# A hybrid decoder layer: the final norm of the prompt rows is moved ahead of the last two expert blocks, and the rows of those two blocks are gathered, normed and stored once more

## The reference

```python
h = x + (gc * conv_out + gg * gla_out) @ w_out
h = h + hier_moe(rms_norm(h, norm_ffn), ...)      # each row goes to TOP_K = 2 of 32 experts
# hier_moe: y = segment_sum(yb * row_wt[:, None], row_tok), expert(x) = (silu(x @ w_g) * (x @ w_u)) @ w_d
y_prompt = rms_norm(hp, norm_final)               # (1, 1024, 1024)
y_sample = rms_norm(hs, norm_final)               # (8, 4, 1024)
# rms_norm(x, g) = x * rsqrt(mean(x * x) + EPS) * g, per row
```

## Time and profile before

| what | value |
|---|---|
| median of 3 runs | 1723.63 us (1722.59 to 1725.98) |
| the profiled execution | 1724.93 us |
| its span | 1723.3 us |
| TensorE busy | 1660.8 us, 96% of the span |
| VectorE (DVE), ScalarE (ACT) busy | 1256.2 us (73%), 922.2 us (54%) |
| GpSimd (POOL) busy | 243.3 us (14%) |
| HBM read, written | 325.19 MB, 61.22 MB |

### The profile page before, as it was taken

One profiled execution on the slowest core, in us unless ns is written; L12 is line 12 of the kernel. 1 busy time (PEld: TensorE's weight loads), 2 busy tenths in 40 slices (PEclk: granted clock), 3 DMA queues, 4 the chain that ended last, 5 costly groups with the idle time before them and its releaser, 6 DMA issues.

```text
span 1723.3 us, 24970 instructions
## 1 busy us (share of the span) xinstructions
PE 1660.8 (96%) x8996; PEld 1461.6 (85%) x8996; DVE 1256.2 (73%) x2086; ACT 922.2 (54%) x1177; POOL 243.3 (14%) x266
## 2 busy tenths in 40 slices
PE   8999999999999999999999989999999999999992
PEld 7999987777999999879988878888888888878881
DVE  5234899986766577645554559998989888888893
ACT  6263122217333344336343347878888887787883
POOL 4100111110000000011001223411111111121210
PEclk9999999999999999999999999999999999999996
DMA  5402223241342333356443339999999999999975
GB/s 202 144 26 75 75 99 109 93 117 54 112 125 92 92 92 116 118 170 202 150 160 111 102 153 368 362 374 368 369 392 384 386 382 395 373 370 378 364 262 208
DMA packets 104033, 367.08 MB, mean 213 GB/s; under 512 B 14509, under 2 KB 58753, under 8 KB 90128
## 3 DMA queue, kind: packets, MB, share of 16 engines
q1 hardware_dynamic: 80976, 308.76, 48.2%
q0 software_dynamic: 22768, 57.19, 10.2%
q10 hardware_dynamic: 208, 0.08, 0.0%
HBM read 325.19 MB, written 61.22 MB: 224 GB/s over the span
## 4 chain that ended last, share of the span: by engine, by line
PE 88%; DMA 5%; DVE 3%; ACT 2%; issue 1%; DVEq 0%; SPq 0%; ACTq 0%; POOLq 0%
PE bank L1023 84%; DMA wraw_down<-in_w_expert_down 3%; PE bank L1478 2%; PE bank L1502 1%; DMA uo<-in_x_prompt 1%; DVE gwork L2030 1%; DMA fbuf<-h_scr 1%; PE bank L1395 0%; PE bank L1242 0%; DMA h_scr<-ybuf,kdT 0%; ACT L1582 0%; DVE wL_down L2030 0%; ACT ybuf L1582 0%; ACTq L1599 0%; DVE fbuf L2673 0%
## 5 line engine op out<-in xcount | busy, mean ns | idle before, releaser
L2030 DVE TENSOR_TENSOR wL_down<-wraw_down,wH_down 128x1024 fp32r<-128x1024 f32 x140 | 162.0, 1218 | 29.7 <-ACT wH_down L1582 29.5
L2030 DVE TENSOR_TENSOR wL_up<-wraw_up,wH_up 128x2048 fp32r<-128x2048 f32 x72 | 161.5, 2284 | 23.9 <-ACT wH_up L1582 23.9
L1582 ACT ACTIVATE wH_up<-wraw_up 128x2048 fp32r<-128x2048 f32 x72 | 134.0, 1909 | 68.3 <-DMA wraw_up<-in_w_expert_up 46.8
L2030 DVE TENSOR_TENSOR wL_gate<-wraw_gate,wH_gate 128x2048 fp32r<-128x2048 f32 x72 | 161.7, 2287 | 11.0 <-ACT wH_gate L1582 10.8
L2155 DVE SCALAR_TENSOR_TENSOR ybuf<-uo,gwork,ybuf 128x1024 f32<-128x1024 f32 x120 | 153.6, 1280 | 6.1 <-issue 6.1
L1582 ACT ACTIVATE wH_down<-wraw_down 128x1024 fp32r<-128x1024 f32 x140 | 136.5, 1052 | 14.1 <-DMA wraw_down<-in_w_expert_down 13.9
L967 POOL DMA_INDIRECT h_scr<-ybuf,kdT x36 | 77.0, 2139 | 436.2 <-ACT ybuf L1582 417.5
L1582 ACT ACTIVATE stage<-bank 128x512 f32<-128x512 f32 (+3 forms) x65 | 34.5, 547 | 189.9 <-PE bank L1023 180.3
L1582 ACT ACTIVATE wH_gate<-wraw_gate 128x2048 fp32r<-128x2048 f32 x72 | 134.5, 1933 | 1.2 <-DMA wraw_gate<-in_w_expert_gate 1.2
L1023 PE MATMUL bank<-nTH,gateH 128*128 128x352 f32 x384 | 129.5, 337 | 0.6 <-issue 0.6
L1023 PE MATMUL bank<-nTH,slabH 128*128 128x352 f32 x384 | 124.9, 325 | 1.2 <-ACT uo L1582 0.7
(11 more groups left out here) (334 smaller groups left out, 4251.6 us busy)
## 6 DMA issues: line engine op xcount, KB each, us to landing
wraw_gate<-in_w_expert_gate SPq DMA_DIRECT2D x36, 2048.0 KB
wraw_up<-in_w_expert_up SPq DMA_DIRECT2D x36, 2048.0 KB, 16.3
wraw_down<-in_w_expert_down SPq DMA_DIRECT2D x36, 2048.0 KB
slab_raw<-in_w_in SPq DMA_DIRECT2D x7, 2048.0 KB, 9.3
gate_scr<-stage POOLq DMA_DIRECT2D x16, 528.0 KB, 3.5
vr_scr<-stage POOLq DMA_DIRECT2D x32, 256.0 KB, 2.3
gate_raw<-in_w_in SPq DMA_DIRECT2D x16, 512.0 KB, 8.7
vrbuf<-vr_scr SPq DMA_DIRECT2D x16, 512.0 KB, 6.9
```

Of the source, the lines that this page charges most:

```text
L1582: return act.activation(out, in_, func, **kw)
L2030: return dve.tensor_tensor(out, x, y, op)
```

## The change

The eight prompt tiles are no longer loaded after everything has been scattered, but as soon as `scatter(n-2)` has landed, n being the last block. At that point the rows lack only what blocks n-1 and n add. They go into the raw gate and up buffers of block n-1, which are spent once its up product is done, are normed there, in `flush`, and are stored from there. The scatters of blocks n-1 and n wait until the eight loads have landed. After both scatters POOL gathers the rows of the last two lists from `h_scr` anew, ACT and DVE norm them, and POOL stores them by list over what was stored before, after the eight stores have landed. The sample rows are loaded, normed and stored once, after `moe_done`. The buffer `fbuf` is gone, and so is the one ACT instruction ahead of the tail that brought in the root's table. The diff, cut to its core:

```diff
+        def prompt_tiles(b):
+            return [wraw[1 - b][k][:, D * q:D * (q + 1)] for k in range(2) for q in range(4)]
+        late_rows = [flat(ybuf)[:, D * k:D * (k + 1)] for k in range(2)]
+        sample_rows = xg[0]
 # SP
             def load_last_down(n, j):
                 sp.wait_ge(ed_done, n - 1)
                 load_w(sp, W_DOWN, expert_of(j), n % 2)
+                tiles = prompt_tiles(n % 2)
+                sp.wait_ge(eu_done, n)
+                sp.wait_ge(y_scattered[n % 2], 16 * (n // 2))
+                for t in range(NCH):
+                    sp.dma_start(tiles[t], h_scr[t * P:(t + 1) * P, :]).then_inc(tile_loaded[t], 16)
+                for t in range(NCH):
+                    sp.wait_ge(f_made, t + 1)
+                    sp.dma_start(o["y_prompt"][0, t * P:(t + 1) * P, :], tiles[t]).then_inc(f_out, 16)
...
             sp.wait_ge(moe_done, 1)
-            for t in range(NT):
-                sp.dma_start(fh[t][0:rows(t), :], h_scr[t * P:t * P + rows(t), :]).then_inc(tile_loaded[t], 16)
-            for t in range(NT):
-                sp.wait_ge(f_made, t + 1)
-                dst = ...
-                sp.dma_start(dst, fo[t][0:rows(t), :]).then_inc(f_out, 16)
+            sp.dma_start(sample_rows[0:S_T, :], h_scr[SEQ:T, :]).then_inc(tile_loaded[NCH], 16)
+            sp.wait_ge(f_out, 16 * NCH)
+            sp.wait_ge(f_made, NT)
+            sp.dma_start(o["y_sample"].rearrange("b s d -> (b s) d"), sample_rows[0:S_T, :]).then_inc(f_out, 16)
             sp.wait_ge(f_out, 16 * NT)
+            sp.wait_ge(listed_rows, 16 * 5)
 # POOL
             def all_scattered(n):
+                for t in range(NCH):
+                    pool.wait_ge(tile_loaded[t], 48)
+                scatter(n - 1)
                 scatter(n)
                 pool.wait_ge(y_scattered[n % 2], 16 * (n // 2 + 1))
                 pool.sem_inc(moe_done, 1)
+                for k in range(2):
+                    pool.indirect_dma_start(out=late_rows[k], in_=h_scr, in_offset=<lst_tok[:, n - 1 + k]>,
+                                            bounds_check=T - 1).then_inc(listed_rows, 16)
+                pool.wait_ge(f_out, 16 * NCH)
+                for k in range(2):
+                    pool.wait_ge(f_made, NT + k + 1)
+                    pool.wait_ge(listed_rows, 16 * (3 + k))
+                    pool.indirect_dma_start(out=o["y_prompt"][0], in_=late_rows[k], out_offset=<the same list>,
+                                            bounds_check=SEQ - 1).then_inc(listed_rows, 16)
             def pool_block(n):
-                scatter(n - 1)
                 if n + 1 < NE:
-                    return
-                if n + 1 < NBLK:
-                    maybe(pool, n_more > n + 1 - NE, pool.nop, lambda: all_scattered(n))
+                    scatter(n - 1)
+                elif n + 1 < NBLK:
+                    maybe(pool, n_more > n + 1 - NE, lambda: scatter(n - 1), lambda: all_scattered(n))
 # ACT
+            def row_roots(x, unread, total, root):
+                r = x.shape[0]
+                f(unread[0:r, :], x, ACT.Square, accum_out=total[0:r, :])
+                act.drain()
+                f(root[0:r, :], total[0:r, :], ACT.Sqrt, scale=1.0 / D, bias=eps_t[0:r, :]).then_inc(rms_made, 1)
                 def flush():
                     weight_high(W_DOWN, b, i * 16 + 16, wH[W_GATE])
                     hidden_high(n, last_hidden(1 - b)[0])
+                    squares(0, 2)
                     last_y()
+                    squares(2, 4)
                     take_y(n, b, i * 16, bank=2)
+                    squares(4, NCH)      # squares: wait for tile_loaded[t], row_roots(prompt_tiles(b)[t], ...)
...
-            f(rstd9[0], eps_t, ACT.Sqrt)
-            for t in range(NT):          # the same three instructions, on fh[t]
+            act.wait_ge(tile_loaded[NCH], 48)
+            row_roots(sample_rows[0:S_T, :], xjunk, ss9[NCH], rstd9[NCH])
+            act.wait_ge(listed_rows, 16 * 3)
+            for k in range(2):
+                row_roots(late_rows[k], xjunk, ss[k], rstd[k])
 # DVE
                 def flush():
...
                     hidden_low(n, last_hidden(1 - b))
+                    dve.wait_ge(norm_row_loaded, 32)
+                    for t in range(NCH):
+                        final_norm(t, prompt_tiles(b)[t], rstd9[t])   # reciprocal, then the product, in place
...
-            for t in range(NT):          # reciprocal and product, fh[t] to fo[t]
+            final_norm(NCH, sample_rows[0:S_T, :], rstd9[NCH])
+            for k in range(2):
+                final_norm(NT + k, late_rows[k], rstd[k])
```

More of the change, by code:

```diff
@@ L201, in hybrid_layer @@
         hidTL = at("hidTL", O_Y + R16 // 2 + KB2, [P, FC, P], FR)
-        fbuf = at("fbuf", O_A, [P, 2, NT, D])
         def flat(t):
@@ L370, in hybrid_layer @@
         ey_taken = sem("ey_taken")
-        more_rows = sem("more_rows")
+        listed_rows = sem("listed_rows")
         y_scattered = [sem(f"y_scattered{b}") for b in range(2)]
@@ L444, in hybrid_layer @@
         cnt = small[:, 32:32 + NE]
-        fh = [fbuf[:, 0, t, :] for t in range(NT)]
-        fo = [fbuf[:, 1, t, :] for t in range(NT)]
+        def prompt_tiles(b):
+            return [wraw[1 - b][k][:, D * q:D * (q + 1)] for k in range(2) for q in range(4)]
+        late_rows = [flat(ybuf)[:, D * k:D * (k + 1)] for k in range(2)]
+        sample_rows = xg[0]
         nfin = mtab[:, :]
@@ L777, in _ @@
             sp.wait_ge(moe_done, 1)
-            for t in range(NT):
-                sp.dma_start(fh[t][0:rows(t), :], h_scr[t * P:t * P + rows(t), :]).then_inc(tile_loaded[t], 16)
-            for t in range(NT):
-                sp.wait_ge(f_made, t + 1)
-                dst = o["y_prompt"][0, t * P:t * P + P, :] if t < NCH else o["y_sample"].rearrange("b s d -> (b s) d")
-                sp.dma_start(dst, fo[t][0:rows(t), :]).then_inc(f_out, 16)
+            sp.dma_start(sample_rows[0:S_T, :], h_scr[SEQ:T, :]).then_inc(tile_loaded[NCH], 16)
+            sp.wait_ge(f_out, 16 * NCH)
+            sp.wait_ge(f_made, NT)
+            sp.dma_start(o["y_sample"].rearrange("b s d -> (b s) d"), sample_rows[0:S_T, :]).then_inc(f_out, 16)
             sp.wait_ge(f_out, 16 * NT)
+            sp.wait_ge(listed_rows, 16 * 5)
             sp.wait_ge(state_out, 4 * 16)
@@ L975, in all_scattered @@
                 pool.sem_inc(moe_done, 1)
+                for k in range(2):
+                    pool.indirect_dma_start(out=late_rows[k], out_offset=None, in_=h_scr,
+                                            in_offset=bass.IndirectOffsetOnAxis(
+                                                ap=lst_tok[:, n - 1 + k:n + k], axis=0),
+                                            bounds_check=T - 1, oob_is_err=False).then_inc(listed_rows, 16)
+                pool.wait_ge(f_out, 16 * NCH)
+                for k in range(2):
+                    pool.wait_ge(f_made, NT + k + 1)
+                    pool.wait_ge(listed_rows, 16 * (3 + k))
+                    pool.indirect_dma_start(out=o["y_prompt"][0], in_=late_rows[k], in_offset=None,
+                                            out_offset=bass.IndirectOffsetOnAxis(
+                                                ap=lst_tok[:, n - 1 + k:n + k], axis=0),
+                                            bounds_check=SEQ - 1, oob_is_err=False).then_inc(listed_rows, 16)
             gather(0)
@@ L985, in _ @@
                                     in_offset=bass.IndirectOffsetOnAxis(ap=m_int[:, 0:1], axis=0)) \
-                .then_inc(more_rows, 16)
+                .then_inc(listed_rows, 16)
             for n in range(NE - 3):
@@ L1985, in flush, with squares @@
                 def flush():
+                    def squares(t0, t1):
+                        for t in range(t0, t1):
+                            act.wait_ge(tile_loaded[t], 48)
+                            row_roots(prompt_tiles(b)[t], xg[b], ss9[t], rstd9[t])
                     weight_high(W_DOWN, b, i * 16 + 16, wH[W_GATE])
                     hidden_high(n, last_hidden(1 - b)[0])
+                    squares(0, 2)
                     last_y()
+                    squares(2, 4)
                     take_y(n, b, i * 16, bank=2)
+                    squares(4, NCH)
                 if nxt:
@@ L2581, in hidden_low, with final_norm @@
                    hidH[:, :, :].rearrange("p k t -> p (k t)").bitcast(F32), ALU.subtract).then_inc(hidT_made, 1)
+            def final_norm(x, rows_of, root):
+                r = rows_of.shape[0]
+                dve.wait_ge(rms_made, 2 * NT + x + 1)
+                dve.reciprocal(root[0:r, :], root[0:r, :])
+                dve.drain()
+                dve.scalar_tensor_tensor(rows_of, rows_of, root[0:r, :], nfin[0:r, :], ALU.mult, ALU.mult) \
+                    .then_inc(f_made, 1)
             def dve_block(n, b, nxt, more, first=False):
@@ L2641, in _ @@
             dve_block(1, 1, True, None)
-            dve.wait_ge(more_rows, 16)
```

(6 more changed lines are left out.)

## The result

The changed kernel takes 1735.51 us (median of 4 runs, 1733.36 to 1736.32), where the kernel before took 1724.52 us on the same chip: a ratio of 1.0067, with a 95% interval of 1.0053 to 1.0080. It is 11 us slower. The prediction was 1724.2 with a range up to 1730.5.

The account below looks back on a forecast made before the run. TensorE bounds the kernel up to the last product, then a copy through full DMA engines. The new chain summed to 1723.5, plus 0.4 for the unseen: span 1723.9, median 1724.2 us, range 1718.0 to 1730.5.

Parts of the forecast that it names:

- step 7: End of program, after the last store by list lands: 0.4 us, giving an end at 1723.5.
- the crowded chain: Rival, chance 0.25: both last scatters slowed beside the stores' backlog; at 9 us each 5.0 us added, 1729.2.
- Where the early loads start: After block 34's up product: scatter(33) lands at 1678.5, first load at 1678.6, all eight tiles there at 1693.8.
- my bounds of 12.7 and 15.2: First issue to eighth landing of the early loads: 12.7 us at the full DMA rate, 15.2 us taken.
- The hidden norms: Early tiles' norms in `flush`: last result delayed 1.7 us at no cost, TensorE's end staying at 1689.1.
- Scatters beside the stores: Last two scatters, scatter(34) beside a backlog of four 512 KB stores: 6.5 us each, to 1701.1 and 1708.5.
- the quiet chain: Rival, chance 0.25: indirect transfers slip through the stores as if alone, loads at full rate; 6.1 us less, span 1717.8.
- an engine takes turns between its queues: Rule for scatter(34) beside stores: DMA engines alternate queues packet by packet, so the backlog is shared, not waited out.
- 2.0 us for each transfer: Rule of fixed cost per GpSimd transfer, plus bytes: an end 6 us earlier; set aside for the trace's durations.
- Gathers, norms, stores: Tail after scatter(35) lands at 1708.5: gathers to 1714.0, two tiles' norms to 1718.6, second store landed at 1723.1.
- the sum: Whole tail: 1723.5 against 1723.3, the copy's 26.2 us becoming a chain of 29.7 that starts 3.3 earlier.

Follow-up runs that it names:

- e2: Kernel before, with POOL made to wait at its program's end until all nine stores have landed: 1735.03 us, ratio 1.0057.
- e9: Kernel before, POOL held until all nine stores landed, plus drains at the head of its blocks from 31 on: 1723.55 us, ratio 1.0000.
- e1: Changed kernel plus one POOL drain after the two gathers are issued: 1728.25 us, ratio 1.0024 to the kernel before.
- e5: Changed kernel plus one POOL drain at the head of all_scattered, before the wait for the eight tiles: 1727.15 us, ratio 1.0029.
- e6: Changed kernel plus one POOL drain after the loop of the first lists, about block 29: 1729.20 us, ratio 1.0039.
- e4: Changed kernel with late rows normed ahead of the sample rows and the root's table loaded beforehand: 1734.62 us, ratio 1.0054.
- e8: Changed kernel with e4's order and e5's drain together: 1726.51 us, ratio 1.0017 to the kernel before.
- e7: e8 plus late gathers and stores behind POOL's absent-block branches, separate gather semaphores, sample rows on ACT's queue: 1720.31 us, ratio 0.9986.

## Why the prediction was wrong, point by point

**The step that failed** is step 7, "End of program 0.4". It took the distance from the last landing to the end from the trace of before, where SP was the last engine. The change makes POOL the last one, with branches still ahead of it and a drain to come. It was 10.4 us (1723.2 to 1733.6, and 0.2 more to the end): 4.2 us from POOL's last work to the drain, of which 1.9 lie ahead of the store's landing, and 8.07 for the drain. Five runs show the drain's part: it can be added to the kernel before (e2), taken away again there (e9), and taken from the changed kernel (e1, e5, and most of it in e6). In the prediction I had weighed who waits behind each of POOL's new waits, and forgot the end of its own program, though the 7902 ns stood in the trace. No rival covered it; the crowded chain, which gave the right sign, was the wrong cause.

**Where the early loads start: right.** Scatter(33) landed at 1676.3 and the first load was issued at 1676.33; from the scatter's start 7.3 us against 8.9 before. The first load landed after 3.71 us, as forecast. The eighth was there 13.3 us after the first issue, not 15.2: the drop in rate was not met again. It was between my bounds of 12.7 and 15.2.

**The hidden norms: right.** TensorE's last matmul started at 1687.01 (1688.70 before), so its end did not suffer, and scatter(35) never waited for ACT.

**Scatters beside the stores: right.** Scatter(34) took 6.0 us and scatter(35) 6.1, with 6.5 and 6.5 forecast. From 1690 to 1698 the DMA engines were full with stores meanwhile:

```profile
1690.00:1698.00 8.00, 0.00 (x0) 0.00 (x0) 5.52 (x8) 4.71 (x12) 2.12 (x2) 0.58 1.03 395
```

Neither the quiet chain (4.5 and 5.7) nor the crowded one (9 or more) came. A backlog of four stores cost scatter(34) 1.5 us and not its own 5 (2.1 MB at 408 GB/s). The rule that the prediction took from the Trainium skill ("DMA: Bandwidth & Descriptors", "Queues, rings and completion order"), that an engine takes turns between its queues, fits this. The other rule, from "Anatomy of one DMA" in the Trainium skill's same page, 2.0 us for each transfer, gives too little for the scatters: 6.0 and 6.1 us less POOL's own 1.5 leave 4.5 and 4.6. For the two stores by list it is close: 3.0 and 2.85 less POOL's 1.4 and 1.0 leave 1.6 and 1.85.

**Gathers, norms, stores: the right steps, but their sum 5.0 us too small.** From scatter(35)'s landing to the last store's were 19.6 us, not 14.6. Four things were missing. The sample rows stood in front on ACT: SP came to their load only at 1706.55, 2.1 us after the first gather, since it too had branches to pass (1697.1 to 1706.4, where the prediction had nothing but the wait for `moe_done`). A second table load of 1.28 us (1711.07) stood between ACT's first square and root, because the one instruction that the diff drops had put both under one table. In e4, which has that instruction again, there is no such load. The second store waits for the first to have landed, `listed_rows` at 16 * 4: the diff says so, and I priced only POOL's own time. So 3.8 us lie between the two starts where I had 1.8. And the second gather landed 4.6 us after its start, not 3.4. This last one was hidden, since ACT was still with the sample rows. Against these, loads and scatters were 2.7 us quicker and the first load went out 2.3 earlier, so that the last landing, forecast for 1723.1, came at 1723.2. That agreement is luck: two errors of 5 us cancelled.

**What the early copy brings** is what the sum said: nearly nothing with its late rows in this order. With the drain gone the kernel is still 0.2 to 0.3% slower than before (e1, e5), where I had forecast no change; by the rows, the missing items above and POOL's branches behind the last store make up that difference. This is argued and not shown: no run takes them out one by one, and e8, without the sample rows in front and without the second table load, gained only 0.6 us by the medians. In e7, where most of them are gone together, the early copy pays.

## What to carry to other kernels

Before you make an engine the last one to end, look at the trace for what its program still does after its last work: branches to pass and the closing drain, which may have been hidden for as long as another engine ended later. A drain of POOL can be had in an idle stretch, ahead of the chain that sets the end; the stretch must be long enough, since beside transfers under way it took 8 to 20 us here. And where a bulk copy is exchanged for a chain of small dependent transfers, price each link from start to landing and then the next issue: here some 3 us for a store by list and 0.9 to issue the next one.

## What the runs showed of the hardware

Where all of POOL's transfers had landed, its drain had a length that went with their number since its last one: 210 and 212 ns after 2, 538 after 6, 1368 after 16, 7902 after 108 and 8065 after 112. It was the same whether they had landed 2.4 us or 26 us before (7902 in the kernel before, 7904 in e2), so there it isn't waiting for data. What else goes with their number, such as their packets, wasn't varied apart from it.

Where a transfer was still under way, the drain lasted at least until it had landed: e7's closing drain of 3120 ns, and in e9 the last of the added ones, of 8373 ns, which began at 1669.9, after scatter(33), and ended at 1678.3, 0.1 us after that landed.

In the kernel before, POOL passed the 13 branches of the absent blocks within 2.3 us, from the last scatter's landing at 1697.0 to its drain at 1699.3. In the changed kernel the same 13 and the way to the drain took 5.4 us, from 1720.1. The branches in the kernel before, then in the changed one (count, ns, first and last start):

```profile
L459 POOLq COMPARE_BRANCH  x13: 41/45/45, 1697.1 to 1699.2; - x13
```

```profile
L462 POOLq COMPARE_BRANCH  x13: 41/45/50, 1720.1 to 1725.4; - x13
```

Two gaps of 1.7 us make the difference, 1721.2 to 1722.9 and 1723.3 to 1725.1, and one packet of the instruction queue was moved in each. The third one below came after the drain had begun (DMA packets, 1721 to 1726):

```profile
q0 software_dynamic: 144, 0.12, 7.4%
q14 instruction: 3, 0.02, 1.7%
```

The Trainium skill ("Runtime: NRT & Kernel Launch", "Instruction fetch mechanics") states that a taken branch whose target isn't in the window already fetched waits for a fetch by DMA; the trace agrees, though no run here isolates one.
